# The RWKV mixer's triangular inverses: packed 64x64 blocks, VectorE turns and corner products

## The reference

```
S = S * w_t - (S kk_t) (kk_t * a_t)^T + v_t k_t^T        # state, 64 x 64
o_t = S r_t
```

## Time and profile before

| | us |
|---|---|
| median of 3 runs | 3352.41 (3349.59 to 3357.58) |
| the profiled execution, its own time | 3355.02 |
| its span, first to last instruction | 3353.3 |
| PE busy in the span | 3154.9 (94%) |
| VectorE busy | 2226.6 (66%) |
| ScalarE busy | 1367.8 (41%) |
| mean granted clock of TensorE | 0.975 |

### The profile page before, as it was taken

The page is one execution under the profiler, slowest core; times in us unless marked ns, Lnnn a source line. Parts: engine busy times, 40 slices in busy tenths (PEclk is TensorE's granted clock), DMA queues, the critical chain, the costliest instruction groups (busy, mean ns, idle before and its releaser), DMA issues.

```text
span 3353.3 us, 46356 instructions
## 1 busy us (share of the span) xinstructions
PE 3154.9 (94%) x18816; PEld 2644.4 (79%) x18816; DVE 2226.6 (66%) x2767; ACT 1367.8 (41%) x1654; POOL 215.9 (6%) x394
## 2 busy tenths in 40 slices
PE   5899999779999999889999999989989899999999
PEld 2588988448888888678888888889877788888887
DVE  2677767477777776457778778758985555555554
ACT  1322311365555555334434444434453343434342
POOL 1000000000000000001212121100000000000000
PEclk9899999889999999799999999999999999999999
DMA  9977987870000021458888888855404555555553
GB/s 324 356 259 248 323 281 246 301 273 11 12 13 12 12 52 24 148 164 285 290 284 291 293 287 296 272 183 183 164 1 138 164 189 188 192 196 186 192 188 126
DMA packets 306001, 640.88 MB, mean 191 GB/s; under 512 B 19035, under 2 KB 23937, under 8 KB 303585
## 3 DMA queue, kind: packets, MB, share of 16 engines
q1 hardware_dynamic: 269280, 529.94, 46.9%
q0 software_dynamic: 28384, 94.76, 8.6%
q10 hardware_dynamic: 8128, 13.24, 1.1%
HBM read 624.33 MB, written 13.40 MB: 190 GB/s over the span
## 4 chain that ended last, share of the span: by engine, by line
PE 86%; DVE 7%; DMA 3%; ACT 2%; issue 1%; ACTq 0%; SPq 0%; POOLq 0%; DVEq 0%
PE ps L441 45%; PE ps L459 14%; PE ps L461 7%; PE ps L1549 6%; DMA raw<-in_ada_w_dram 3%; PE ps L1592 3%; PE ps L2210 2%; PE ps L378 1%; PE ps L1646 1%; PE ps L1603 1%; DVE rw_scl L1269 1%; DVE rw_scc L1272 1%; PE ps L1481 1%; DVE line L748 1%; PE ps L1616 1%
## 5 line engine op out<-in xcount | busy, mean ns | idle before, releaser
L406 ACT ACTIVATE split_hi<-raw 128x2048 fp32r<-128x2048 f32 x368 | 702.2, 1912 | 1176.6 <-PE ps L441 838.1
L418 DVE TENSOR_TENSOR split_lo<-raw,split_hi 128x2048 fp32r<-128x2048 f32 (+1 forms) x372 | 849.7, 2285 | 500.3 <-ACT split_hi L406 490.5
L459 PE MATMUL ps<-xa,split_hi 128*128 128x512 f32 x2048 | 723.5, 398 | 6.5 <-ACT xa L613 6.5
L461 PE MATMUL ps<-xa,split_lo 128*128 128x256 f32 x2048 | 574.0, 280 | 0.0
L459 PEld LDWEIGHTS ps<-xa,split_hi 128*128 128x128 f32 x2048 | 384.7, 188 | 103.1 <-ACT xa L613 7.4
L441 PE MATMUL ps<-split_hi,hT_hi 128*128 128x512 f32 x1024 | 399.6, 390 | 0.0
L441 PE MATMUL ps<-split_hi,hT_lo 128*128 128x512 f32 x1024 | 398.5, 389 | 0.0
L441 PE MATMUL ps<-split_lo,hT_hi 128*128 128x512 f32 x1024 | 398.4, 389 | 0.0
L461 PEld LDWEIGHTS ps<-xa,split_lo 128*128 128x128 f32 x2048 | 386.5, 189 | 0.2
L441 PEld LDWEIGHTS ps<-split_hi,hT_hi 128*128 128x128 f32 x1024 | 192.2, 188 | 41.5 <-issue 1.8
L441 PEld LDWEIGHTS ps<-split_hi,hT_lo 128*128 128x128 f32 x1024 | 192.2, 188 | 40.3
(11 more groups left out here) (367 smaller groups left out, 4868.8 us busy)
## 6 DMA issues: line engine op xcount, KB each, us to landing
raw<-in_mlp_w_dram SPq DMA_DIRECT2D x256, 1024.0 KB, 5.4
raw<-in_ada_w_dram SPq DMA_DIRECT2D x64, 1024.0 KB, 9.5
raw<-in_mix_in_w_dram SPq DMA_DIRECT2D x48, 1024.0 KB, 5.9
raw<-in_conv_pw_w_dram SPq DMA_DIRECT2D x48, 1024.0 KB, 5.2
gate<-in_ada_w_dram SPq DMA_DIRECT2D x172, 256.0 KB, 4.9
line<-in_ada_w_dram POOLq DMA_DIRECT2D x171, 256.0 KB, 5.0
late<-in_ada_w_dram POOLq DMA_DIRECT2D x85, 256.0 KB, 5.1
tmpa<-in_ada_w_dram SPq DMA_DIRECT2D x84, 256.0 KB, 4.9
```

The source lines that it names most:

```text
L406: nc.scalar.activation(split_hi[:, c, :, 0:n], raw[:, c, :, 0:n], ACT.Copy).then_inc(hi_done, 1)
L418: nc.vector.tensor_tensor(split_lo[:, c, :, 0:n], raw[:, c, :, 0:n], split_hi[:, c, :, 0:n], ALU.subtract).then_inc(lo_done, 1)
L459: pe.matmul(ps[:, base + j, :], split_hi[:, c, kk, j * P:(j + 1) * P], both, start=(k == 0), stop=False, skip_group_check=True)
L461: mm = pe.matmul(ps[:, base + j, 0:SEQ], split_lo[:, c, kk, j * P:(j + 1) * P], xa_hi[:, k, :], start=False, stop=(k == KT - 1), skip_grou ...
```

## The change

An inverse of 128x128 is taken apart into its two diagonal blocks of 64x64 and the corner that couples them. The diagonal blocks of two chunks (8 instances, 16 blocks) are packed in one tile of 128x512, so that there are two tiles b = 0, 1 in the place of four chunks. Six levels make NS = 12 rounds k = 2*level + b.

- ACT packs the tiles from the masked scores (`packed`, two instructions of 64 partitions each). PE opens the value's bank with them by a product with the unit matrix (`opened`).
- In a round DVE masks straight from PSUM and, in the ten rounds of the first five levels, turns the mask's result itself: `V.transpose` turns each 32x32 block, which suffices as these levels couple nothing beyond 32. ACT copies the value for the next product beside it (`level_values`). `update` is now 16 matmuls of 64x64 by 64 columns, each half of the partitions by itself.
- The last level couples 32 with 32 and is turned on PE by matmuls with the unit matrix (`turn_last`) and copied by ACT.
- The corner is Z1 (N Z2), two products of 64x64: `corners` makes the negated, turned scores anew from the keys, `corner_half` the first product, `corner_turn` turns one factor, `corner` makes the second, after the scan's first `inputs_of`. DVE and ACT write the results to `tt` (`corner_out`); its other corners stay zero from one memset at the start.
- The fillers of DVE move to other rounds; `shift_value` comes after the corners. `rh` and `u` share a tile with `nt`, `zt` and `gz` lie in `mb`. The scores' banks are ordered anew. Some semaphores are joined.

```diff
 LAM_INIT = 0.8 - 0.6
-LEVELS = 7
+LEVELS = 6
+HB = P // 2
...
+    late("mb", P, 2, 8, HB)
+    late("mt", P, 2, 8, HB)
+    late("zz", P, 2, 8, HB)
     late("tt", P, 4, 4, P)
-    late("rh", P, 4, HD)
-    late("u", P, 4, HD)
+    late("ru", P, 2, 4, HD)
     late("sp", P, 2, 2, HD)
     late("o", P, SEQ)
+        t["rh"], t["u"], t["nt"] = t["ru"][:, 0, :, :], t["ru"][:, 1, :, :], t["ru"]
+        t["zt"], t["gz"] = t["mb"][:, :, 0:4, :], t["mb"][:, :, 4:8, :]
         at = attention_memory(nc)
     return t, at
...
-    "bon_ps", "g_ps", "y", "bv", "khd")}
-        ZB, MB = [0, 1, 2, 3], [6, 7]
-        NS = 4 * LEVELS
-        SCB = [7, 2, 6, 0, 1, 3, 7, 2, 6, 0, 7, 1, 2, 3, 1, 2]
+    "cum_ps", "cum", "v", "prod", "tr_ps", "tr", "sc_ps", "sc", "mb", "mt_d", "mbt_ps", "mt_a", "z_lev", "zz", "off_ps", "off_a", "off_d", "th", "th1",
+    "rh_ps", "rh", "u_ps", "u", "o_ps", "o", "st_ps", "sp", "epi_ps", "om", "sqo", "pr",
+    "g_ps", "y", "bv", "khd")}
+        ZB, MB, GB, NTB = [0, 3], [7, 4], [6, 2], [4, 7]
+        NT_DVE = 2 * (LEVELS - 1)
+        NS = 2 * LEVELS
+        SCB = [7, 2, 6, 0, 1, 3, 4, 7, 2, 6, 1, 3, 4, 7, 2, 6]
+        late_half = lambda d: slice((1 - d) * HB, (2 - d) * HB)
+        own_half = lambda d: slice(d * HB, (d + 1) * HB)
+        def pair_scores(b):
+    return rw["scl"] if b else rw["scc"]
         TRB = [3, 6, 0, 1, 3]
         EPI = 5
...
+    def packed(x, b):
+        act.wait_ge(W["sc"], x.n(16, 8 * b + 8))
+        for e in range(2):
+            h = own_half(e)
+            ins = nc.scalar.activation(rw["zz"][h, b, :, :].rearrange("p (i c) s -> p i c s", c=2),
+                                       pair_scores(b)[h, :, :, h].rearrange("p c i s -> p i c s"), ACT.Copy)
+        ins.then_inc(W["zz"], 1)
...
+    def corners(x, h):
+        act.wait_ge(W["off_ps"], x.n(8, h + 1))
+        nc.scalar.activation(rw["nt"][:, h, :, :], ps[:, NTB[h], 0:4 * HB].rearrange("p (c s) -> p c s", c=4), ACT.Copy,
+                             scale=-1.0).then_inc(W["off_a"], 1)
+    def level_values(x, k):
+        act.wait_ge(W["mb"], x.n(NT_DVE, k + 1))
+        nc.scalar.activation(rw["zz"][:, k % 2, :, :], ps[:, ZB[k % 2], :].rearrange("p (j s) -> p j s", s=HB), ACT.Copy).then_inc(W["zz"], 1)
+    def last_turned(x, b):
+        act.wait_ge(W["mbt_ps"], x.n(2, b + 1))
+        nc.scalar.activation(rw["mt"][:, b, :, :], ps[:, MB[b], :].rearrange("p (j s) -> p j s", s=HB), ACT.Copy).then_inc(W["mt_a"], 1)
+    def own_blocks(x, b):
+        act.wait_ge(W["z_lev"], x.n(NS, NS - 1 + b))
+        for e in range(2):
+            h = own_half(e)
+            ins = nc.scalar.activation(rw["tt"][h, 2 * b:2 * b + 2, :, h].rearrange("p c i s -> p i c s"),
+                                       ps[h, ZB[b], :].rearrange("p (i c s) -> p i c s", c=2, s=HB), ACT.Copy)
+        ins.then_inc(W["zz"], 1)
...
+    def corner_out(x, b):
+        act.wait_ge(W["off_ps"], x.n(8, 7 + b))
+        nc.scalar.activation(rw["tt"][own_half(1), 2 * b:2 * b + 2, 2:4, late_half(1)].rearrange("p c i s -> p i c s"),
+                             ps[own_half(1), GB[b], 0:4 * HB].rearrange("p (i c s) -> p i c s", c=2, s=HB), ACT.Copy).then_inc(W["off_a"], 1)
...
-        for k in range(NS):
-            act.wait_ge(W["z7_ps"], x.n(NS, k + 1))
-            nc.scalar.activation(rw["tt"][:, k % 4, :, :], four(ZB[k % 4]), ACT.Copy).then_inc(W["z7"], 1)
-            n = k + 2
-            if 4 <= n < NS:
-                act.wait_ge(W["mbt_ps"], x.n(NS, n + 1))
-                nc.scalar.activation(rw["mx"][:, n % 2, :, :], four(MB[n % 2]), ACT.Copy).then_inc(W["mx"], 1)
+        packed(x, 0)
+        packed(x, 1)
+        corners(x, 0)
+        corners(x, 1)
+        for k in range(NT_DVE):
+            level_values(x, k)
+        last_turned(x, 0)
+        last_turned(x, 1)
+        own_blocks(x, 0)
+        own_blocks(x, 1)
+        half_product(x, 0)
+        half_product(x, 1)
+        corner_out(x, 0)
+        corner_out(x, 1)
     def scan(x, last):
...
-        lev, c = k // 4, k % 4
-        if k < 4:
-            dve.wait_ge(W["sc"], x.n(16, 4 * c + 4))
...
+        m = bc(rw["lmask"][:, lev, :, :], 4)
...
-        if k >= 2:
-            dve.wait_ge(W["mbt_ps"], x.n(NS, k - 1))
-        V.tensor_tensor(dh(rw["mb"][:, k % 2, :, :]), dh(src), bc(rw["lmask"][:, lev, :, :], 2), ALU.mult).then_inc(W["mb"], 1)
...
+            dve.wait_ge(W["z_lev"], x.n(NS, k - 1))
+            V.tensor_tensor(out, ps[:, ZB[b], :].rearrange("p (d j s) -> p d j s", d=2, s=HB), m, ALU.mult).then_inc(W["mb"], 1)
+            dve.wait_ge(W["mb"], x.n(NT_DVE, k - 1))
+        if lev < LEVELS - 1:
+            V.transpose(rw["mt"][:, b, :, :].rearrange("p j s -> p (j s)"), rw["mb"][:, b, :, :].rearrange("p j s -> p (j s)")).then_inc(W["mt_d"], 1)
+    def turned_blocks(x, b):
+        dve.wait_ge(W["off_ps"], x.n(8, 4 + 2 * b))
+        V.tensor_copy(rw["zt"][:, b, :, :], ps[:, MB[b], 0:4 * HB].rearrange("p (j s) -> p j s", s=HB)).then_inc(W["off_d"], 1)
+    def corner_out(x, b):
+        dve.wait_ge(W["off_ps"], x.n(8, 7 + b))
+        V.tensor_copy(rw["tt"][own_half(0), 2 * b:2 * b + 2, 0:2, late_half(0)].rearrange("p c i s -> p i c s"),
+                      ps[own_half(0), GB[b], 0:4 * HB].rearrange("p (i c s) -> p i c s", c=2, s=HB)).then_inc(W["off_d"], 1)
...
@@ -1343,45 +1412,50 @@
             if c == 0 and not first:
                 centred(x.last())
         masked(x, 0)
-        masked(x, 1)
         mask_scores(x, 3)
-        for k in range(4):
-            with_unit(x, k)
-            masked(x, k + 2)
...
             masked(x, k)
             if not first:
-                if k < 8:
-                    group_scale(x.last(), k - 6)
...
+                    group_scale(x.last(), 1)
+                elif k == 2:
                     normalised(x.last())
-                elif k == 9:
+                elif k == 3:
...
+            if k == 6:
                 bonus_sum(x)
-            elif k == 13:
+            elif k == 7:
...
-                    shift_key(x.next(), k - 16)
-                elif 19 <= k < 21:
-                    shift_query(x.next(), k - 19)
-                elif k == 22:
-                    shift_query(x.next(), 2)
-                elif 23 <= k < 26:
-                    dve.wait_ge(W["bv"], x.n(1, 1))
-                    shift_value(x.next(), k - 23)
+                elif k == 10:
+                    shift_key(x.next(), 0)
+                    shift_query(x.next(), 0)
+                elif k == 11:
+                    shift_key(x.next(), 1)
+                    shift_query(x.next(), 1)
+        if not last:
+            shift_key(x.next(), 2)
+            shift_query(x.next(), 2)
+        turned_blocks(x, 0)
+        turned_blocks(x, 1)
+        corner_out(x, 0)
+        corner_out(x, 1)
+        if not last:
+            dve.wait_ge(W["bv"], x.n(1, 1))
+            for part in range(3):
+                shift_value(x.next(), part)
     def scan(x, last):
...
+    steps.link(V.memset(rw["tt"][:, :, :, :], 0.0))
...
+    def opened(x, b):
+        pe.wait_ge(W["zz"], x.n(NS + 2, b + 1))
+        free_of_scores(x, ZB[b])
+        pe.matmul(ps[:, ZB[b], :], ident[:, :], R["zz"][:, b, :, :].rearrange("p j s -> p (j s)"), start=True, stop=False, skip_group_check=True)
...
+    def corners(x, h):
+        free_of_scores(x, NTB[h])
+        for c in range(4):
+            for d in range(2):
+                t = SCAN[d][c]
+                mm = pe.matmul(ps[late_half(d), NTB[h], c * HB:(c + 1) * HB], R["kx"][half(h), d, t, 0, late_half(d)],
+                               R["bh"][half(h), d, t, own_half(d)], start=(c == 0), stop=True, skip_group_check=True)
+        mm.then_inc(W["off_ps"], 1)
     def update(x, k):
-        c = k % 4
-        if k < 4:
-            pe.wait_ge(W["mx0"], x.n(4, k + 1))
-            free_of_scores(x, ZB[c])
+        b = k % 2
+        if k < NT_DVE:
+            pe.wait_ge(W["mt_d"], x.n(NT_DVE, k + 1))
         else:
-            pe.wait_ge(W["mx"], x.n(NS - 4, k - 3))
-            pe.wait_ge(W["z7"], x.n(NS, k - 3))
-        for inst in range(4):
-            rhs = R["tt"][:, c, inst, :] if k >= 4 else scores_of(c)[:, inst, 0:P]
-            mm = pe.matmul(ps[:, ZB[c], inst * P:(inst + 1) * P], R["mx"][:, k % 2, inst, :], rhs,
-                           start=(k < 4 and inst == 0), stop=True, skip_group_check=True)
-        mm.then_inc(W["z7_ps"], 1)
+            pe.wait_ge(W["mt_a"], x.n(2, b + 1))
+        pe.wait_ge(W["zz"], x.n(NS + 2, k + 1))
+        for j in range(8):
+            for e in range(2):
+                mm = pe.matmul(ps[own_half(e), ZB[b], j * HB:(j + 1) * HB], R["mt"][own_half(e), b, j, :], R["zz"][own_half(e), b, j, :],
+                               start=False, stop=True, skip_group_check=True)
+        mm.then_inc(W["z_lev"], 1)
...
+    def turn_last(x, b):
+        pe.wait_ge(W["off_a"], x.n(6, 2))
+        pe.wait_ge(W["mb"], x.n(NT_DVE, NT_DVE - 1 + b))
```

(112 more changed lines are left out.)

55 lines of the change are left out of this document (27 added, 28 removed).

## The result

The changed kernel takes 3268.77 us, median of four runs (3263.43 to 3274.67), beside 3354.99 for the kernel before on the same chip: a ratio of 0.9748, 95% interval 0.9729 to 0.9768, 86 us less. The forecast was 3335, 17 to 20 us less. The direction was right and the range (3243 to 3374) holds the time, but the change is worth over four times what I gave it. The case that came true is the first rival, "clock stays" (3248), less 21 us.

The account below looks back on a forecast made before the run. TensorE was taken to bound the inverse (37.2 us of a pass). Saving 12.8 us per pass less 10.8 for a low clock left 2, 16 in eight; with the ends, a gain of 17 gave 3335 us, range 3243 to 3374.

Parts of the forecast that it names:

- the first rival, "clock stays": TensorE stays at 2.4 GHz, 12.8 us saved per pass, 3248 us; chance 0.33 with either price of turn or update.
- the clock: TensorE falls to 1.2 GHz about half-way through the inverse's loop in passes 1 to 6, costing 10.8 us a pass.
- +1.9, +6.8 and +2.1 us a pass, 10.8 of the 12.8 saved: Low clock's price in rest of loop, tail and scan, total 10.8, against 12.8 saved per pass at kept clock.
- 40% idle: TensorE's idle share in the new loop, with two updates of 0.93 us in each level.
- a fall behind one-row matmuls (L2234): Earlier trace, 2505.5 to 2509.4: clock fell with TensorE busy 3.34 of 3.90 us; taken as small pieces not carrying it.
- VectorE as the new bound: In the inverse's loop VectorE sets the pace, 3.2 to 3.4 us a level, and two tiles hide TensorE's rounds.
- The turn, "about 0.63": A VectorE turn of 128x512 in the loop takes about 0.63 us, 0.55 felt when the next instruction is independent.
- Reciprocals felt as 1.7: In the opening, VectorE's two reciprocals, 2 x 0.94 us, are no longer in TensorE's shadow and cost 1.7.
- Update at 0.029 a record: In the loop, an update's 32 records take 0.93 us on TensorE, 1.1 until the last result.
- masked(0) to the first product: First mask to first L1646 in a pass: 45.6 us becomes 32.8 with the clock kept, 41.5 with it low.
- The slower one (3408): Low clock holds from mid-loop through the scan, 7.3 us lost per pass; 0.22 together with low clock and dear turns.
- The dear turn (1.23): VectorE's loop turn costs 1.23 us: 3296 at kept clock (within the 0.33), 3367 at low clock (within the 0.22).

Follow-up runs that it names:

- e2: After with each update's 32 records using 32 rows by 32 columns of the array instead of 64 by 64 (inverses wrong): 3298.2 us.
- after: The changed kernel itself, as against the kernel before at 3354.99 us: 3268.77 us, ratio 0.9748.
- e1: After with half of the matmuls left out of each update of the inverse (inverses wrong): 3271.6 us.
- e3: After with the 32-block turn on VectorE issued twice in each of its 10 places in a pass: 3332.5 us.
- e9: e4 plus later shifts, diagonal-block copies split between ScalarE and VectorE, tiles packed by chunk, VectorE's blocks before its last shifts, one rates matmul before the corners: 3249.2 us.
- e10: e9 with 8 more quarter-size corner matmuls (0.47 us), the same result made twice, before TensorE's wait for tile 1: 3241.1 us.
- e4: After with chunk 3's scores issued before tile 0's copy on TensorE, and VectorE's reciprocals moved before masked(0) and masked(1): 3254.2 us.
- e8: After with the turns of k = 2 to 9 on TensorE, copied by ScalarE, each behind the update its mask waits for: 3389.4 us.
- e11: e8 with the turns in pairs on TensorE, ordered turn(k), turn(k+1), update(k), update(k+1): 3310.4 us.

## Why the prediction was wrong, step by step

**The step that failed is the clock**: "I expect it to fall to 1.2 GHz about half-way through the loop", with +1.9, +6.8 and +2.1 us a pass, 10.8 of the 12.8 saved. Measured: 1.00 through loops and tails, and 3.4 us at 0.50 in four openings, some 1.2 us each, 5 us in all for my 86. Three things were wrong in it.

- The comparison of busy shares. I put the new loop at "40% idle" from the time between issues of 2 x 0.93 in a level, beside the earlier trace rows, whose columns count matmuls to their ends. In those columns the loop is 18.77 of 23.00 busy, above the 2.84 of 4.00 behind which the clock fell. Like was not compared with like. Even so the share could not have decided it: the other fall of the earlier trace rows stands behind 3.34 of 3.90.
- Where the border lies. Quarter pieces do count less (e2), but after keeps the clock with 16 of them an update, and e1 loses it with eight. From a fall behind one-row matmuls (L2234) nothing followed for pieces of 64 rows.
- The price. Where the clock fell in a loop, VectorE hid part of it and the clock was mostly back before the scan: e2's worst pass paid 6.0, not 10.8, and e1's paid one to two by the estimate above. The one pass whose low stretch ran from the tail through the scan (e3's seventh) paid 14.8, more than the 10.8: a fall of that length is dear, but after has none in its middle passes.

A rule of the Trainium skill (TensorE: Matmul & The Clock Gate, Why this matters for your kernels), no long idle gaps between bursts, came out nearer for after than my inference from one row. e9 against e10 agrees with it in kind, though the waits of 1.3 to 1.8 us ahead of the low stretches are shorter than the gap that the page's table names. e2 does not agree: its longest idle time in the 4.9 us ahead of the fall is 0.61 us. So gaps are not all that matters, and what made after hold the clock stays open.

**The other steps.** VectorE as the new bound: right (e3). The turn, "about 0.63": 0.71 from start to end, 0.63 until the next instruction starts (893.75 to 894.38), where I had 0.55. Reciprocals felt as 1.7: 1.64. Update at 0.029 a record, 1.1 until the last result: 1.15. masked(0) to the first product: 34.2 for 32.8. Of the 1.4, 1.1 are in the opening, where my 6.3 for the first two masks and turns was 7.4: packing took 1.33 of wait for 1.1 to 1.2, and I had missed that chunk 3's scores would stand behind opened(0) on TensorE (0.80). The wait for packed(0), 0.45 ahead of masked(0), was missed too. With the 1.4 that is 1.9 a pass, 15 in eight; e4 won 14.5 back. The tail from the last mask (912.2) to 921.19 is 9.0, as worked out. First to fourth product: 16.5 (921.12 to 937.62), the kept-clock end of "16.5 to 19". 12.8 - 1.9 is the 10.9 saved in an undisturbed pass, 87.3 in eight. The first pass saves 2.5 more, the last 5.2 more, mostly since its scan began at full clock, and the low openings take 4.7 back: 90.2. Of the 91.5 of the spans 1.3 lie outside the passes, where the memset (1.8) stands too.

**The rivals.** The slower one (3408) did not come true: in after the low clock never reached a middle scan. Its price was of the right kind: e3's seventh pass lost 14.8 us in tail and scan, where the rival had 8.7 and 11.4 for loop, tail and scan. The dear turn (1.23) was excluded by the first row of L1352.

## What to carry to other kernels

When a change moves work off the engine that bounds a kernel, count the new bound engine's waits in the opening and the tail, not in the loop alone: here a new order on TensorE and one on VectorE, no faster instruction, gave 14.5 us. When you argue on the clock, compare rows in one and the same column, price a fall only where its engine is on the path, and don't let one unlike row outweigh the rows that resemble the new code; where the clock is lost behind a short wait, it can pay to put harmless matmuls ahead of that wait (8 us here). When two matmuls lie on different halves of the array's rows, keep them side by side. And when a turn goes to TensorE, order the tiles so that no matmul stands right behind the one its mask waits for: 79 us between e8 and e11.
